# Differential attention taken head by head, with query and gate tiles between its units and half of the output projection in its last steps

## The reference, cut to what matters

```python
proj = h @ w_in_b                                   # 1024 -> 1024 queries, 1024 gates
q = rope(proj[..., :1024]);  gate = proj[..., 1024:]  # 8 heads, 2 halves of 64
# k_shared (rotated) and v_shared come from the layer's kv projection
sc = q . k * 64 ** -0.5, for each half; masked by chunks of 64 tokens (block-causal)
p = softmax(sc);  w = p[half 0] - lam * p[half 1]
o = w @ v                                           # 8 heads of 128
o = rmsnorm over a head's 128 channels (o) * sub_norm * (1 - lambda_init)
y = (o * silu(gate)) @ w_out_b                      # 1024 -> 1024
x = x + rmsnorm(y, post_norm)
```

## Time and profile before

| | |
|---|---|
| median of 3 runs | 2649.44 us (2644.94 to 2652.12) |
| the profiled execution | 2651.0 us, span of its instructions 2649.2 us |
| mean granted TensorE clock | 0.968 |
| busy share of the span: PE, PEld, DVE, ACT, POOL | 94%, 73%, 46%, 39%, 36% |
| chain that ended last | PE 88%, DVE 6%, ACT 3% |

### The profile page before, as it was taken

The page is one execution under the profiler, slowest core; times in us unless marked ns, Lnnn a source line. Parts: engine busy times, 40 slices in busy tenths (PEclk is TensorE's granted clock), DMA queues, the critical chain, the costliest instruction groups (busy, mean ns, idle before and its releaser), DMA issues.

```text
span 2649.2 us, 32653 instructions
## 1 busy us (share of the span) xinstructions
PE 2484.0 (94%) x11250; PEld 1926.7 (73%) x11252; DVE 1207.1 (46%) x2591; ACT 1042.6 (39%) x1714; POOL 955.9 (36%) x780
## 2 busy tenths in 40 slices
PE   6999999989999989999998999988999989799877
PEld 4667767778888867776777888876788767577555
DVE  7565664654344366557465344134300340534562
ACT  5544434334443244544423444223223442333662
POOL 1234222334444443322243444452444434244211
PEclk9999999989999999999999999999999999899988
DMA  7532123412226253113341222222222202122100
GB/s 257 195 140 79 38 92 114 157 64 95 95 85 225 87 191 127 64 36 97 123 146 70 101 96 80 99 85 74 90 96 98 100 17 83 49 91 80 64 1 32
DMA packets 51728, 259.13 MB, mean 98 GB/s; under 512 B 6112, under 2 KB 16096, under 8 KB 26016
## 3 DMA queue, kind: packets, MB, share of 16 engines
q1 hardware_dynamic: 50464, 249.26, 27.1%
q0 software_dynamic: 1152, 8.39, 0.9%
HBM read 249.11 MB, written 7.34 MB: 97 GB/s over the span
## 4 chain that ended last, share of the span: by engine, by line
PE 88%; DVE 6%; ACT 3%; issue 2%; DMA 1%; POOL 0%; SPq 0%; ACTq 0%; DVEq 0%; POOLq 0%
PE bank L617 24%; PE bank L619 23%; PE bank L618 23%; PE bank L708 3%; PE bank L732 2%; PE bank L721 1%; PE bank L674 1%; PE bank L1045 1%; PE bank L974 1%; PE bank L649 1%; PE bank L843 1%; DMA bias_scratch<-stage 1%; PE bank L1118 1%; PE bank L1034 1%; PE bank L1137 1%
## 5 line engine op out<-in xcount | busy, mean ns | idle before, releaser
L543 POOL TENSOR_TENSOR w_lo<-w_raw,w_hi 128x512 fp32r<-128x512 f32 (+1 forms) x700 | 883.0, 1292 | 1434.4 <-ACT w_hi L1191 887.7
L617 PE MATMUL bank<-h_hi,w_hi 128*128 128x512 f32 x1792 | 734.7, 410 | 32.9 <-DVE h_lo L2054 14.3
L619 PE MATMUL bank<-h_hi,w_lo 128*128 128x512 f32 x1792 | 704.2, 393 | 0.0
L618 PE MATMUL bank<-h_lo,w_hi 128*128 128x512 f32 x1792 | 703.2, 392 | 0.0
L617 PEld LDWEIGHTS bank<-h_hi,w_hi 128*128 128x128 f32 x1792 | 340.2, 190 | 130.6 <-issue 62.3
L618 PEld LDWEIGHTS bank<-h_lo,w_hi 128*128 128x128 f32 x1792 | 340.1, 190 | 72.6 <-issue 8.4
L619 PEld LDWEIGHTS bank<-h_hi,w_lo 128*128 128x128 f32 x1792 | 339.1, 189 | 73.4
L1191 ACT ACTIVATE w_hi<-w_raw 128x2048 fp32r<-128x2048 f32 (+1 forms) x108 | 189.7, 1757 | 280.4 <-PE bank L619 245.5
L2012 DVE SCALAR_TENSOR_TENSOR cv<-bank,par,cv 128x511 f32<-128x511 f32 (+1 forms) x176 | 131.7, 749 | 215.2 <-ACT cv L1440 202.3
L1440 ACT ACTIVATE cv<-bank,par 128x512 f32<-128x512 f32 x88 | 68.3, 779 | 235.3 <-PE bank L619 235.3
L1196 ACT ACTIVATE w_hi<-w_raw 128x2048 fp32r<-128x2048 f32 x76 | 145.1, 1909 | 35.9 <-PE bank L619 35.9
(11 more groups left out here) (344 smaller groups left out, 3761.0 us busy)
## 6 DMA issues: line engine op xcount, KB each, us to landing
w_raw<-w_stream SPq DMA_DIRECT2D x150, 1024.0 KB, 4.8
w_raw<-w_down SPq DMA_DIRECT2D x32, 704.0 KB, 4.1
ada_mid<-w_ada SPq DMA_DIRECT2D x20, 1024.0 KB, 6.9
ada_last<-w_ada SPq DMA_DIRECT2D x12, 1024.0 KB, 4.8
ada_early<-w_ada POOLq DMA_DIRECT2D x8, 1024.0 KB, 8.1
ada_late<-w_ada SPq DMA_DIRECT2D x8, 1024.0 KB, 6.7
bias_in<-bias_scratch SPq DMA_DIRECT2D x16, 256.0 KB, 2.6
bias_in<-bias_scratch SPq DMA_DIRECT2D x16, 192.0 KB, 2.3
```

The lines of the kernel that those rows point to most:

```text
L543: ins = nc.gpsimd.tensor_tensor(w_lo[r][:, part], w_raw[r][:, part], w_hi[r][:, part].bitcast(fp32), ALU.subtract)
L617: nc.tensor.matmul(out, w[0][:, cols], xh, start=first, stop=False)
L618: nc.tensor.matmul(out, w[0][:, cols], xl, start=False, stop=False)
L619: return nc.tensor.matmul(out, w[1][:, cols], xh, start=False, stop=last)
```

## The change

Only the last layer changes.

- The units run head by head: heads = (i, h) with i innermost, so each head has rounds of 128, 256, 384 and 512 keys.
- Only query tiles 0 and 1 stand ahead of the rounds. The other six query tiles and all eight gate tiles, 14 tiles in the order MIX, have their steps in the 32 rounds, four and three in turn (mix_step). They all use bank 3. The weights of the query and gate slots are put in that order on the host. The swaps of query tiles 2 to 7 stand at the start of the rounds 4, 6, 13, 15, 22, 24 (bank 2).
- The value product is taken turned: v is the stationary operand and the result has a head's 128 channels on partitions and the tokens in columns, four units of a head in one bank. ScalarE copies it to q2 and squares it (head_out), in rounds 7, 11, 15, ..., 31 and after. The 32 transposes, O2 and yd go.
- The mean over a head's channels is now over partitions. TensorE sums the squares by token (head_squares, four matmuls of one column). VectorE and ScalarE make the factor of each token (head_tokens, head_roots, head_scales), VectorE writes it on a diagonal (head_diagonal, four operations), TensorE spreads it to all partitions (head_spread), VectorE multiplies (head_gated, head_scaled), ScalarE and GpSimd split the product to yh2 and yl2.
- Heads 0 to 3 go through this in rounds 20 to 29, heads 4 to 7 after the rounds.
- The output projection has eight banks. Tiles 0 to 3 take k 0 to 3 first (heads 0 to 3), then k 4 to 7; tiles 4 to 7 follow whole. The sums of squares stand behind tiles 4 to 7.

```diff
@@ plan @@
-        BESIDE.append([[(1 + s // KD, s % KD) for s in range(4 * u, 4 * u + 4)] for u in range(14)])
+        BESIDE.append(beside([4, 3] * H * 2, [(j, k) for j in range(14) for k in range(KD)]))
+        heads = [(i, h) for h in range(H) for i in range(NB)]
+        MIX = [("q", 2), ("q", 3), ("g", 0), ("g", 1), ("q", 4), ("q", 5), ("g", 2), ("g", 3), ("q", 6), ("q", 7),
+               ("g", 4), ("g", 5), ("g", 6), ("g", 7)]
+        SWAP_AT = {4: 2, 6: 3, 13: 4, 15: 5, 22: 6, 24: 7}
+        SPREAD_AT = [23, 25, 26, 27]
@@ GpSimd @@
+            for h in range(4):
+                head_lo(h)
+            lo_loop(slot_no(2, SLOT2_OUTB), 2, SLOT)
+            for h in range(4, H):
+                head_lo(h)
@@ TensorE @@
+            def mix_step(j, k):
+                m, t = SLOT2_Q2 + 1 + j // 2, TILE2_Q2 + 2 + j
                 if k == 0:
                     wait_slot(2, m)
-                    wait_bank(2, t, 2)
+                    wait_bank(2, t, 1)
+                ins = mm3(banks[3][:, :], split(2, m), slice((j % 2) * D + k * P, (j % 2) * D + (k + 1) * P),
...
+            def head_squares(h):
+                pe.wait_ge(o_evac, UB + h + 1)
+                if h:
+                    pe.wait_ge(otok_read, h)
+                by_token(2, osq[h % 2], ones).then_inc(otok_done, 1)
+
+            def head_spread(h, bank):
+                pe.wait_ge(dg_ready, h + 1)
+                nc.tensor.matmul(banks[bank][:, :], ones, dg[h % 2][:, :], start=True, stop=True).then_inc(spread_done, 1)
...
-                        ins = nc.tensor.matmul(banks[u % 2][:, 0:P], PT2[u % 2][:, b * P:(b + 1) * P],
-                                               v2[:, b, h * P:(h + 1) * P], start=(b == 0), stop=(b == i))
+                        ins = nc.tensor.matmul(banks[h % 2][:, i * P:(i + 1) * P], v2[:, b, h * P:(h + 1) * P],
+                                               PT2[u % 2][:, b * P:(b + 1) * P], start=(b == 0), stop=(b == i))
...
+            pe.wait_ge(logit, UB + 2 * NU)
+            wait_slot(2, SLOT2_OUTB)
+            out_b((0, 1), range(4))
+            pe.wait_ge(ry_mul, NB * H + 4)
+            head_squares(7)
+            pe.wait_ge(pt_evac, UB + NU)
+            wait_slot(2, SLOT2_OUTB + 1)
+            out_b((2, 3), range(4))
+            pe.wait_ge(otok_read, H)
+            wait_bank(2, TILE2_OUTB, 1)
+            for h in range(4, H):
+                if h >= 6:
+                    pe.wait_ge(ry_mul, NB * H + h - 1)
+                head_spread(h, 2 + h % 2)
+            out_b((0, 1), range(4, KD))
+            out_b((2, 3), range(4, KD))
...
+            for f in range(4, KD):
                 if f % 2 == 0:
                     wait_slot(2, SLOT2_OUTB + f // 2)
...
+                out_b((f,), range(KD))
+                for s in {4: (0, 1), 5: (2, 3), 6: (4,), 7: (5, 6, 7)}[f]:
+                    square_sum(s)
@@ ScalarE, round t @@
+            for t in range(NU + 4):
+                j = next((j for j, k in BESIDE[3][t - 1] if k == KD - 1), None) if 1 <= t <= NU else None
+                if j is not None:
+                    kind, h = MIX[j]
+                    act.wait_ge(tile_done, tdone(2, TILE2_Q2 + 2 + j))
+                    A_(q2[:, h, :] if kind == "q" else g2[:, h, :], banks[3][:, :], ACT.Copy).then_inc(tile_evac, 1)
...
+                if j is not None and j % 2:
+                    split_hi(2, SLOT2_Q2 + 1 + j // 2 + 2)
+                if t >= 7 and t % 4 == 3:
+                    head_out(t // 4 - 1)
+                if t == 21:
+                    head_gates(0)
+                    head_roots(0)
+                if t - 2 in SPREAD_AT:
+                    head_hi(SPREAD_AT.index(t - 2))
+                if t == NU + 1:
+                    head_gates(1)
@@ VectorE, after the rounds @@
+            for h in range(4, 7):
+                head_gated(h)
+            head_tokens(7)
+            head_scales(1)
+            head_diagonal(4)
+            head_diagonal(5)
+            head_gated(7)
+            head_scaled(4, 2)
+            head_diagonal(6)
+            head_scaled(5, 3)
+            head_diagonal(7)
+            head_scaled(6, 2)
+            head_scaled(7, 3)
```

More of the change, by code:

```diff
@@ new lines, in _ @@
+                if t >= 8 and t % 4 == 0:
+                    pe.wait_ge(qk_ready, 2 + 24 + 2 + len([s for s in SWAP_AT if s <= t]))
+                    pe.wait_ge(ry_mul, NB * H + len([b for b in SPREAD_AT if b < t]))
+                    head_squares(t // 4 - 2)
+                if t in SPREAD_AT:
+                    pe.wait_ge(qk_ready, 2 + 24 + 2 + len([s for s in SWAP_AT if s <= t]))
+                    pe.wait_ge(otok_read, len([h for h in range(H) if 4 * h + 8 <= t]))
+                    pe.wait_ge(ry_mul, NB * H + SPREAD_AT.index(t))
+                    head_spread(SPREAD_AT.index(t), 2)
@@ new lines, in out_b @@
+            def out_b(fs, ks):
+                for k in ks:
+                    pe.wait_ge(ry_lo, NB * H + k + 1)
+                    for f in fs:
+                        cols = slice((f % 2) * D + k * P, (f % 2) * D + (k + 1) * P)
+                        ins = mm3(banks[4 + f if f < 4 else f - 4][:, :], split(2, SLOT2_OUTB + f // 2), cols,
+                                  yh2[:, k, :], yl2[:, k, :], k == 0, k == KD - 1)
+                        if k == KD - 1:
+                            ins.then_inc(tile_done, 1)
@@ L1155, in _, with square_sum @@
+            out_b((0, 1), range(4, KD))
+            out_b((2, 3), range(4, KD))
             e0 = KD * (2 * DEPTH + 3)
[L1156 removed]
+            def square_sum(f):
+                pe.wait_ge(sq_ready, e0 + f + 1)
+                stat(ones, 4, sq[f % 2][:, :], f).then_inc(sq_used, 1)
+            for f in range(4, KD):
                 if f % 2 == 0:
                     wait_slot(2, SLOT2_OUTB + f // 2)
[L1159 to L1168 removed]
@@ L1547, in _ @@
             take_h(2, range(4, KD))
-            raw_loop(SLOT2_Q2, TILE2_Q2, 4, q2)
+            for q in range(2):
+                evac(2, TILE2_Q2 + q, q2[:, q, :]).then_inc(tile_evac, 1)
+            split_hi(2, SLOT2_Q2 + 2)
             act.wait_ge(lam_ready, 1)
```

255 lines of the change are left out of this document (126 added, 129 removed).

## The result

The change makes the kernel slower: a median of 2659.39 us (2656.64 to 2663.55, seven runs) against 2650.72 us (2644.94 to 2652.81, seven runs) of the kernel before. The ratio is 1.0038, with a 95% interval of 1.0025 to 1.0052. The forecast was 2648.5 us and "no change". The profiled execution of the changed kernel took 2663.55 us and ties for the slowest of its seven, 4 us above their median; its span is 2661.5 us.

What follows compares the result with a forecast made beforehand. TensorE was taken as the bound, with 45.4 us of waits and half clock. From 2391.9, 204.2 us of work and 34.4 of waits end at 2630.5 instead of 2631.4, so 2648.5 us; 8-in-10 range 2638 to 2662.

Steps and rivals of the forecast that it cites:

- place 1: Start, before the first scores: TensorE idles 3.9 us, plus 0.7 for a clock that may have fallen, 4.6 in all.
- places 2 and 7: Mixed tiles sharing one bank, and slot 50 before output tile 4; TensorE's clock there costs 1.3 us together.
- Rival B: Slower: TensorE's clock falls at one-bank waits, about 2 us each, ten giving 2667 us; chance 0.24 together with other late chains.
- one-bank ends: Ten mixed tiles end inside a round; the next step waits until ScalarE empties bank 3: 17.5 us lost.
- place 3: Round 21's ScalarE work, Silu of 2048 columns and three table loads: 6.0 us, meeting TensorE only in round 22's 1.6.
- added work: On TensorE, eight token sums (6.6) and eight spreads (7.3) come, 32 transposes of O (3.8) go: +10.1 us.
- Places 4 to 7: TensorE waits at first spreads 2.8, end of rounds 1.6, second half of the heads 3.4, slot 50 3.0 us.
- place 7: Slot 50 is ready 9.1 us after output tile 0's end, other tiles cover 6.1: 3.0 us lost.
- Place 6: Second half of the heads: TensorE waits 1.9 us between spreads, plus 1.5 for GpSimd holding VectorE off.
- rival C: GpSimd holds VectorE off: eight diagonal operations of heads 6 and 7 give +8 us, 2657; chance included in 0.54.
- The case named as likeliest: The prediction's sum, with rival C: within 0.3% (8 us), no change that shows; own range 2642 to 2657; chance 0.54.
- the case given 0.24: Rival B and other late chains, such as a slot not ready, more than 9 us in all; chance 0.24.

Runs made afterwards that it cites:

- e1_relax: The changed kernel, but the swap of query 1 no longer waits for the rotation of query 0; 2659.37 us, ratio 1.0031 to the kernel before.
- e6_start: e3_ends with query 1's swap moved to the start of round 1 and the lambda reductions ahead of query 0's rotation; 2637.30 us, 0.9950 to the kernel before.
- e11: The changed kernel run once more, unaltered; 2661.53 us, ratio 1.0036 to the kernel before.
- e3_ends: The changed kernel with mixed steps respread so that no mixed tile ends inside a round; 2641.82 us, ratio 0.9965 to the kernel before.
- e7_order: The changed kernel, but in rounds 11 and 27 ScalarE copies the ended mixed tile ahead of head_out; 2658.58 us, ratio 1.0036 to the kernel before.

## Why the prediction was wrong, by its own steps

**The start (place 1, 4.6 us) missed a wait, and with it 4.4 us.** The text said "Both swaps run, then the first scores need rotated query 1". They don't both run: the changed code lets swap_q(1, 5) wait for the rotation of query 0, so swap, rotation, swap, rotation stand in a row on two engines. (Before, a swap waited for the rotation two back, and a whole query tile stood between two swaps.) The wait is 2.2 us, the second swap at half clock costs 1.1 more (2.05 against 0.91), round 0 1.7 (5.30 instead of 3.64); of these 5.0 the place had 0.7 for the clock. The wait before the first scores, 3.9 by the text, was 3.64. e1_relax gave 2.9 back, e6_start 5.6.

**The clock (0.7 in place 1 and 1.3 for places 2 and 7) was mis-sized.** The term of 1.3 rested on one row, where 3.08 us of idle time left the clock up. The rounds and the tail lose 4.9 + 3.8 = 8.7 us to it (8.5 by five falls at 1.7), 7.4 more than counted. With the start's 4.4 that is 11.8 of the 13.2 us. The other 1.4 us are not assigned to a step: three waits that no place of the sum had (0.32 before a swap, 0.51 before transposes, 0.36 before a token sum) come to 1.2 us, but the idle times of places 4 to 7 came out shorter than said, by more than that. And the 13.2 us are those of the profiled execution; another profile of the same kernel (e11) has 2.3 less. Rival B said 2 us a fall, against 1.7 measured, and its five falls came, but only two of them at the one-bank waits, rounds 22 and 27: the seven shorter one-bank waits never brought the clock down, while a token sum's wait, the spreads and slot 50 often did. The Trainium skill (TensorE: Matmul & The Clock Gate, A second HAM failure mode: psum-queue depth-cycling) also tells of a kernel that cycles through PSUM banks and whose many small idle times between groups of matmuls are enough to throttle it again and again; the traces agree in kind (five falls behind the start, with waits of 1.57 to 3.38 us just ahead of them).

**The one-bank ends (17.5 us) were right**, in sum and nearly one by one: 0.95 to 1.05 for the five short ones (1.04 said), 1.93 for round 2 (1.85 said), 3.04 and 3.55 for rounds 11 and 27 (3.1 and 3.7), 1.86 and 2.23 for rounds 20 and 22 (2.0 and 1.6). e3_ends took them away and gave 22.0 us with their clock. That ScalarE's order makes rounds 11 and 27 the worst is shown by e7_order: it takes away 0.98 and 1.48 of their 2.87 and 3.38 us.

**Round 21 (place 3, 6.0 us)** took 6.1 (2509.07 to 2515.20). ScalarE's timeline there, Silu of half the gates and the load behind it:

```profile
2510.36 1.91 ACT L1627 ACTIVATE g<-g 128x2048 f32<-128x2048 f32 x1
...
2512.29 1.28 ACT L1631 ACT_TABLE_LOAD   x1
```

The load starts at once behind the Silu (2510.36 + 1.91 = 2512.27), as in the earlier trace rows. The 1.38 us of drain that the Trainium skill gives beside each load (ScalarE: Activation LUTs, What ACT_TABLE_LOAD costs) don't show here either.

**The added work (+10.1)** holds as far as it was tried: the eight token sums a second time cost 6.5 us (6.6 said). The spreads were not tried alone.

**Places 4 to 7** came out a little shorter than said, in idle time: 0.23, 0.83 and 1.57 (2.8 said) around the first spread, 0.73 (1.6) at the end of the rounds, 0.80 and 1.81 (3.4) before the last spreads, 2.57 (3.0) for slot 50. The parts named in place 7 add up to 8.9 and not to the 9.1 written there, and its copies took 1.65 of the 1.9. Place 6 had GpSimd's hold on VectorE in it, and rival C did not come: one diagonal, four operations, took 2.39 us, 1.5 more than alone, where C had eight operations 1.05 longer each.

**The direction.** The change was put at -0.9 us, where terms of 10 to 50 us cancel, so the missed 13 decided it. The case named as likeliest reached to 2657, and the measured 2659.4 lies above it. What came is the case given 0.24, late chains and falls of the clock of more than 9 us in all, and its sign, the clock falling in the rounds, was among those named. That 2659.4 lies within the wide range of 2638 to 2662 says little for the working: the two missed steps used up nearly all of it.

## What to carry to other kernels

When stages are interleaved so that a tile can end anywhere, count the engines between a tile's last matmul and the next tile on the same bank: one line of the plan that put the ends between rounds was worth 17.6 us of the median and turned a loss into a gain. In a chain of short operations between two engines, read every wait of the new code in order; the one between two swaps that "both run" cost 2.2 us and more again in clock. Where TensorE waits in dense work, price a fall of the clock (1.7 us here, once 3.4) behind some of the waits instead of taking the one row that shows none, and think of filling a wait with matmuls of no use.
